# A written order of every stage in a slot of the attention heads, the rotated key's halves among the value projections, and a finer order in the odd mixer

## What is computed

```python
def mla_attend(qn, qr, kn, kr, v):            # kind A, 8 heads; kr is one rotated key for all heads
    s = einsum('bqhd,bkhd->bhqk', qn, kn) + einsum('bqhr,bkr->bhqk', qr, kr)
    p = softmax(s * scale)
    return einsum('bhqk,bkhe->bqhe', p, v)
def diff_attend(q1, q2, k1, k2, v, lam):      # kind B, 4 heads
    p = softmax(s1) - lam * softmax(s2)
    return einsum('bhqk,bkhe->bqhe', p, v)    # then rms_norm per head
for l in range(2):                            # first block
    o_a = mla_attend(lat, keys of ctx and lat); o_b = diff_attend(...)
    # in layer 0 the context's queries attend to the context too
    merged = sigmoid(ga) * (o_a @ w_br_a) + sigmoid(gb) * (rms_norm(o_b) @ w_br_b)
    x = x + gate * (merged @ w_out); x = x + gate * conv_ffn(x)
# second block: layer 0 an even mixer, layer 1 the odd mixer:
#   z = h @ w_in; compressed attention + causal attention in two branches, gated; retention; @ w_out
```

## Time and profile before

| | us |
|---|---|
| median of 3 runs | 3557.78 |
| lowest, highest | 3555.96, 3561.11 |
| profiled execution | 3556.24 |
| its span in the trace | 3554.5 |
| PE busy in it | 3348.7 |
| DVE, ACT, POOL busy | 1958.8, 1402.4, 324.9 |
| mean granted TensorE clock | 0.977 of full |

### The profile page before, as it was taken

The page is one execution under the profiler, slowest core; times in us unless marked ns, Lnnn a source line. Parts: engine busy times, 40 slices in busy tenths (PEclk is TensorE's granted clock), DMA queues, the critical chain, the costliest instruction groups (busy, mean ns, idle before and its releaser), DMA issues.

```text
span 3554.5 us, 42096 instructions
## 1 busy us (share of the span) xinstructions
PE 3348.7 (94%) x17348; PEld 2799.1 (79%) x17348; DVE 1958.8 (55%) x2880; ACT 1402.4 (39%) x2281; POOL 324.9 (9%) x269
## 2 busy tenths in 40 slices
PE   8889998999999998899899999899999989989998
PEld 5778777888888886787777888787888767768886
DVE  5675655677736635757645635555444466344343
ACT  4563443234313324544534423444222356243222
POOL 0010000221101110000011101221000210210000
PEclk9999999999999998999999999999999999999999
DMA  5001114443323322011143322222222311112222
GB/s 222 30 23 63 42 50 163 138 144 120 113 88 125 131 77 83 19 52 59 62 143 119 130 100 94 97 95 86 91 105 85 112 38 36 60 59 99 97 98 74
DMA packets 74608, 321.94 MB, mean 91 GB/s; under 512 B 9008, under 2 KB 17968, under 8 KB 52400
## 3 DMA queue, kind: packets, MB, share of 16 engines
q1 hardware_dynamic: 74416, 319.25, 25.9%
HBM read 303.49 MB, written 15.73 MB: 90 GB/s over the span
## 4 chain that ended last, share of the span: by engine, by line
PE 50%; DVE 5%; ACT 3%; issue 1%; POOL 0%; DMA 0%; DVEq 0%; ACTq 0%; POOLq 0%; SPq 0%
PE psum L688 14%; PE psum L689 14%; PE psum L690 14%; PE psum L1291 1%; DVE split_weights L658 1%; PE psum L1323 1%; ACT split_weights L640 1%; DVE arena L2158 0%; ACT arena L1437 0%; PE psum L703 0%; PE psum L3005 0%; PE psum L704 0%; PE psum L705 0%; PE psum L2590 0%; PE psum L3029 0%
## 5 line engine op out<-in xcount | busy, mean ns | idle before, releaser
L688 PE MATMUL psum<-split_inputs,split_weights 128*128 128x512 f32 (+1 forms) x2864 | 1053.8, 368 | 20.4 <-DVE split_weights L658 17.3
L689 PE MATMUL psum<-split_inputs,split_weights 128*128 128x512 f32 (+1 forms) x2864 | 1045.6, 365 | 0.0
L690 PE MATMUL psum<-split_inputs,split_weights 128*128 128x512 f32 (+1 forms) x2864 | 1044.8, 365 | 0.0
L658 DVE TENSOR_TENSOR split_weights<-arena,split_weights 128x2048 fp32r<-128x2048 f32 (+6 forms) x324 | 513.2, 1599 | 423.2 <-ACT split_weights L640 422.0
L688 PEld LDWEIGHTS psum<-split_inputs,split_weights 128*128 128x128 f32 x2864 | 543.3, 190 | 114.8 <-DVE split_weights L658 21.9
L689 PEld LDWEIGHTS psum<-split_inputs,split_weights 128*128 128x128 f32 x2864 | 543.1, 190 | 87.3 <-issue 2.8
L690 PEld LDWEIGHTS psum<-split_inputs,split_weights 128*128 128x128 f32 x2864 | 542.3, 189 | 87.0
L640 ACT ACTIVATE split_weights<-arena 128x2048 fp32r<-128x2048 f32 (+6 forms) x327 | 423.9, 1314 | 163.7 <-PE psum L690 163.6
L688 PE MATMUL psum<-split_hidden,split_weights 128*128 128x512 f32 (+1 forms) x880 | 324.3, 368 | 2.4 <-DVE split_weights L658 2.4
L689 PE MATMUL psum<-split_hidden,split_weights 128*128 128x512 f32 (+1 forms) x880 | 324.0, 368 | 0.0
L690 PE MATMUL psum<-split_hidden,split_weights 128*128 128x512 f32 (+1 forms) x880 | 323.8, 368 | 0.0
(11 more groups left out here) (354 smaller groups left out, 4773.1 us busy)
## 6 DMA issues: line engine op xcount, KB each, us to landing
arena<-w_up_dram SPq DMA_DIRECT2D x44, 1024.0 KB, 5.5
arena<-ffn_up_dram SPq DMA_DIRECT2D x44, 1024.0 KB, 4.8
arena<-w_ada_dram SPq DMA_DIRECT2D x80, 512.0 KB, 3.8
arena<-w_in_dram SPq DMA_DIRECT2D x32, 1024.0 KB, 4.8
arena<-w_down_dram SPq DMA_DIRECT2D x32, 704.0 KB, 4.1
arena<-ffn_down_dram SPq DMA_DIRECT2D x32, 704.0 KB, 4.1
arena<-od_w_in_dram SPq DMA_DIRECT2D x13, 1024.0 KB, 4.8
arena<-w_ada_dram SPq DMA_DIRECT2D x8, 1024.0 KB, 12.3
```

The lines of the kernel that those rows point to most:

```text
L658: ins = dve.e.tensor_tensor(ws[:, i, 1, cols], raw_view(key)[:, cols], ws[:, i, 0, cols].bitcast(F32), ALU.subtract)
L688: pe.e.matmul(dst, a[0], b[0], start=i == 0, stop=False)
L689: pe.e.matmul(dst, a[0], b[1], start=False, stop=False)
L690: ins = pe.e.matmul(dst, a[1], b[0], start=False, stop=i == n - 1)
```

## The change

1. `SLOT_ORDER` gives, for each layer, kind and engine, the order of twelve stages in a slot, and the loop in `head_items` follows it. Against the order before: in layer 0, kind A, PE does `values` before `turn`, ACT does `values` before `turn` and the first scores' exponential after the pieces, DVE does the pieces last. In layer 0, kind B, PE does `turn` before the first scores, DVE weighs before the first maximum and splits weights before the pieces. In layer 1, kind A, ACT does `values` before `turn`, DVE weighs first. In layer 1, kind B, PE does `ob_sum` after values, gates and pieces.
2. `PIECE_SHIFT` moves single pieces by one slot: in layer 0 both key projections of kind A one later, the latent key projection of the last three heads of kind B one earlier; in layer 1 the latent key projection of kind A one later and the context's one earlier. `GATE_AT` moves some gates by one or two slots.
3. `KRF` moves into a row of `PR`. The halves of the rotated key become four items `kr`, one behind each of the first four `v_a`, on ACT and DVE; the two waits for them ahead of L1544 go, and ACT waits for the taken latent before it writes `KRF`.
4. Odd mixer: DVE's split of the second query block moves ahead of `dve_blocks`; in `nsa_order` the weight blocks are split in quarters, one a slot, and the first of them no longer stands before the first scores; PE does `fill` ahead of `values`.

The diff. Of the loop over the slots only the first of the removed lines stand here; the rest of them are in the kernel before, printed above. Of `PIECE_SHIFT` the further entries are left out: they repeat the named ones for the other heads.

```diff
--- before.py
+++ after.py
@@ -250,8 +250,25 @@
-GATE_AT = {2: ((3, 4, 6, 7), (10, 11, 13, 14), (17, 18, 19, 20), (21, 23, 24, 26)),
-           1: ((3, 5), (7, 9), (11, 13), (15, 17))}
+GATE_AT = {2: ((3, 4, 7, 7), (10, 11, 14, 14), (17, 18, 19, 20), (22, 24, 25, 27)),
+           1: ((1, 3), (6, 9), (12, 14), (15, 17))}
+SLOT_ORDER = {
+    (0, "A", "act"): ("late", "ob_sum", "values", "turn", "ob_root", "gates", "pieces", "s0", "preps", "s1", "ob_norm", "ob_square"),
+    (0, "A", "dve"): ("s0", "late", "weigh", "turn", "ob_sum", "values", "ob_root", "gates", "preps", "s1", "pieces", "ob_norm", "ob_square"),
+    (0, "A", "pe"): ("s0", "values", "turn", "late", "ob_sum", "ob_root", "gates", "pieces", "preps", "s1", "ob_norm", "ob_square"),
+    (0, "B", "act"): ("turn", "late", "ob_sum", "values", "s0", "ob_root", "gates", "pieces", "preps", "s1", "ob_norm", "ob_square"),
+    (0, "B", "dve"): ("weigh", "s0", "late", "turn", "ob_sum", "values", "preps", "ob_root", "gates", "pieces", "s1", "ob_norm", "ob_square"),
+    (0, "B", "pe"): ("turn", "s0", "late", "ob_sum", "values", "ob_root", "gates", "preps", "s1", "pieces", "ob_norm", "ob_square"),
+    (1, "A", "act"): ("late", "ob_sum", "values", "turn", "s0", "ob_root", "gates", "pieces", "preps", "s1", "ob_norm", "ob_square"),
+    (1, "A", "dve"): ("weigh", "s0", "late", "turn", "ob_sum", "values", "ob_root", "gates", "pieces", "preps", "s1", "ob_norm", "ob_square"),
+    (1, "A", "pe"): ("s0", "turn", "late", "ob_sum", "values", "ob_root", "gates", "pieces", "preps", "s1", "ob_norm", "ob_square"),
+    (1, "B", "act"): ("turn", "late", "ob_sum", "values", "s0", "ob_root", "gates", "pieces", "preps", "s1", "ob_norm", "ob_square"),
+    (1, "B", "dve"): ("s0", "late", "weigh", "turn", "ob_sum", "values", "ob_root", "gates", "pieces", "preps", "s1", "ob_norm", "ob_square"),
+    (1, "B", "pe"): ("s0", "turn", "late", "values", "ob_root", "gates", "pieces", "ob_sum", "preps", "s1", "ob_norm", "ob_square"),
+}
+PIECE_SHIFT = {(0, 1, 2): 1, (0, 1, 3): 1, (0, 10, 3): -1,
...
@@ -358,7 +375,8 @@
         for i, step in enumerate(steps):
-            plan[lo + i * (hi - lo) // len(steps)]["pieces"].append(step)
+            x = lo + i * (hi - lo) // len(steps) + PIECE_SHIFT.get((layer, n, i), 0)
+            plan[x]["pieces"].append(step)
@@ -370,7 +388,10 @@
         if i == len(streams):
-            out += [("v_a", t) for t in range(N_TOK // P)]
+            for t in range(N_TOK // P):
+                out.append(("v_a", t))
+                if engine != "pe" and t < 4:
+                    out.append(("kr", t // 2, t % 2))
         out += step
@@ -390,42 +411,47 @@
+    def part_preps(n):
+        out.extend(preps[0:n])
+        del preps[0:n]
     for x, (i, c) in enumerate(slots):
         scores = plan[x]["scores"]
-        if engine != "act":
-            out += scores[0:1]
...
+        for stage in SLOT_ORDER[layer, pairs[i]["kind"], engine]:
+            if stage == "s0":
+                out += scores[0:1]
+            elif stage == "s1":
+                out += scores[1:]
+            elif stage == "late":
+                out += late
+                late = []
+            elif stage == "weigh":
+                out += [("weigh", t) for t in weigh]
+                weigh = []
+            elif stage == "turn":
+                out.append(("turn", i, c))
+            elif stage == "values":
+                if len(values) > 2:
+                    of_values(x, *values.pop(0))
+            elif stage == "gates":
+                if gates[x] and gates[x][0][2:] == (LAT, 0):
+                    part_preps(len(preps))
+                out += [y for y in gates[x] if y[0] != "prepare"]
+                preps += [("prepare", part, PARTS) for y in gates[x] if y[0] == "prepare" for part in range(PARTS)]
+                late += [("gate_out",) + y[1:] for y in gates[x] if y[0] == "gate"]
+            elif stage == "pieces":
+                for step in plan[x]["pieces"]:
+                    if step[0][0] == "v_b" or step[0][0] == "b_qk" and step[0][3:] == (0, LAT):
+                        part_preps(len(preps))
+                    out += [y for y in step if y[0] != "prepare"]
+                    late += [("late",) + y for y in step if y[0] in ("a_q", "a_k")]
+                    preps += [("prepare", part, PARTS) for y in step if y[0] == "prepare" for part in range(PARTS)]
+            elif stage == "preps":
+                part_preps(2)
+            else:
+                of_norm(x, stage)
+        weigh += [t for _, t in scores]
     out += late + preps
@@ -1033,7 +1059,7 @@
         OS_HI = spare(2 * P)
-        KRF = arena[:, region:region + N_TOK]
+        KRF = PR[:, 2, :]
         VB = Layout(arena, half_n0, arena_n)(6, H_B, 2 * P, words=split_words)
@@ -1105,14 +1131,9 @@
             act.wait_ge(product, "kr", l, CTX)
+            act.wait_ge(taken, "cq", l, 2, mine(l)[-1])
             act.e.activation(KRF[kr, CTX[0]:CTX[1]], banks.at("kr", l, CTX)[kr, 0:N_CTX], ACT.Copy,
                              scale=kc("scale_a")[kr, :]).then_inc(*banks.back(("kr", l, CTX), copied, "kr", l, CTX))
-            act.wait_ge(roped, l, "kr")
-            act.wait_ge(copied, "kr", l, CTX)
-            for b in range(2):
-                for at in (kr, kr2):
-                    act.e.activation(KH[at, b, 0, :], KRF[kr, :], ACT.Copy, scale=1.0 / a_scale).then_inc(
-                        *w_half("kr", l, b, at.start))
             act.wait_ge(const_in)
@@ -1145,12 +1166,6 @@
             dve.e.tensor_tensor(KRF[kr, lat], KRF[kr, lat], KT[kr, :], ALU.add).then_inc(*roped(l, "kr"))
-            for b in range(2):
-                for at in (kr, kr2):
-                    dve.wait_ge(w_half, "kr", l, b, kr.start)
-                    dve.e.scalar_tensor_tensor(out=KH[at, b, 1, :], in0=KRF[kr, :], scalar=1.0 / a_scale,
-                                               in1=KH[kr, b, 0, :].bitcast(F32), op0=ALU.mult, op1=ALU.subtract).then_inc(
-                        *taken("kr", l, b, at.start))
@@ -1396,6 +1411,12 @@
                                      ACT.Copy).then_inc(*w_half("k", l, n, s))
+                elif what == "kr":
+                    b, rows = at[0], (kr, kr2)[at[1]]
+                    act.wait_ge(roped, l, "kr")
+                    act.wait_ge(copied, "kr", l, CTX)
+                    act.e.activation(KH[rows, b, 0, :], KRF[kr, :], ACT.Copy, scale=1.0 / a_scale).then_inc(
+                        *w_half("kr", l, b, rows.start))
                 elif what == "v_a":
@@ -1538,8 +1559,6 @@
                         qt_free()
-                        dve.wait_ge(taken, "kr", l, 1, kr2.start)
-                        dve.wait_ge(w_half, "kr", l, 1, kr2.start)
                         dve.wait_ge(product, "q", l, n, s)
@@ -1560,6 +1579,12 @@
                                         ).then_inc(*banks.back(("k", l, n, s), taken, "k", l, n, s))
+                elif what == "kr":
+                    b, rows = at[0], (kr, kr2)[at[1]]
+                    dve.wait_ge(w_half, "kr", l, b, kr.start)
+                    dve.e.scalar_tensor_tensor(out=KH[rows, b, 1, :], in0=KRF[kr, :], scalar=1.0 / a_scale,
+                                               in1=KH[kr, b, 0, :].bitcast(F32), op0=ALU.mult, op1=ALU.subtract).then_inc(
+                        *taken("kr", l, b, rows.start))
                 elif what == "v_a":
@@ -2738,11 +2763,14 @@
-        def dve_odd_in(chunks):
+        def dve_odd_in(chunks, ready=0):
             block, waiting = None, []
                 if b != block:
-                    dve_prepare()
+                    if ready == 0:
+                        dve_prepare()
+                    ready = max(ready - 1, 0)
                     block = b
@@ -2958,7 +2986,8 @@
             pieces = [("fill", c, j) for c in range(len(RET_IN)) for j in range(4)]
-            out, late, evict = [("cmp_scores",), ("prepare",)], [], []
+            out, late, evict = [("cmp_scores",)], [], []
+            preps = [("prepare", part, PARTS) for part in range(PARTS)]
             for x in range(min(at.values()), len(chunk_list) + 2):
@@ -2968,17 +2997,18 @@
                     slot["fill"].append(pieces.pop(0))
-                late, evict = [], []
+                late, evict = preps[0:1] if x > -3 else [], []
+                preps = preps[len(late):]
                 for _, c, j in slot["fill"]:
                         evict += [("fill_out", c)]
-                        late += [("prepare",)] * (c % 2)
-                order = dict(pe="scores turn cmp values fill", dve="scores weigh turn cmp values late",
+                        preps += [("prepare", part, PARTS) for part in range(PARTS * (c % 2))]
+                order = dict(pe="scores turn cmp fill values", dve="scores weigh turn cmp values late",
                              act="evict turn values scores weigh cmp late")[engine]
             assert not pieces
-            return out + evict + late
```

(8 more changed lines are left out.)

32 lines of the change are left out of this document (1 added, 31 removed).

## The result

The changed kernel took 3501.9 us (median of 4 runs, 3493.8 to 3504.3) beside 3558.7 of the kernel before: ratio 0.984, 95% interval [0.982, 0.985], 56.8 us less. Run once more beside later experiments, it took 3498.0 (3491.5 to 3504.5), ratio 0.983 [0.981, 0.985], 60.8 us less. The forecast was 3507.5, in a range of 3486 to 3537.

A forecast was written before the change was run, and what follows sets the result against it. PE, busy 94% of the span, bounds the kernel, so only its waits and clock count. Terms summed to 57 us, 50 after counting the heads' 20.5 at two thirds: 3557.8 to 3507.5 us, range 3486 to 3537.

The forecast's parts named there:

- Key halves, -11.5: Starts of both layers' heads: moving KRF frees DVE's queue, so scores start 6.0 and 5.5 us sooner, -11.5 us.
- A of layer 0, -6: Layer 0's heads of kind A: the turn's wait for its weighing mostly goes in seven heads, -6 us.
- B of layer 0, -7: Layer 0's heads of kind B: shorter waits of scores (2.4), norm sums (3.9) and gates (0.7), -7 us.
- Layer 1, -4.5 and -3: Layer 1's heads: in kind A the turn's wait goes, -4.5 us; in kind B the norm sum's is covered, -3.
- Rival B: Re-ordered heads lose over half of their 73 us of idle time, 38.5, at full clock: 3483 us; chance 0.12.
- (a): Odd mixer's queries: the weight split moved ahead of the copies removes PE's wait of 4.63 us for L658, -4.6 us.
- (b): Odd mixer's first scores: without the whole block ahead of the first maximum, the 5.24 us wait shrinks to 0.8, -4.4 us.
- (c): Odd mixer's attention: fill ahead of values and quartered blocks cut PE's waits for the output bank, -8.1 us.
- The clock, -8: PE's granted clock recovers where long waits go: 5 us in the odd mixer, 3 in the heads, -8 us.
- A of the rivals: Only the starts, the odd mixer and 5 us of clock gain; the heads' re-orderings give nothing: 3524 us; chance 0.25.
- C: Heads: ACT blocks on evictions and scores wait for their bank, 2.8 us a head in 24 heads: 3591 us; chance 0.05.
- D: Moved split and fill meet the next wait at once; starts and odd mixer give half, the rest nothing: 3541; chance 0.09.

The follow-up runs named there:

- gates_back: The changed kernel with the gates back in their old slots in both layers, orders and moved pieces kept: 3510.2 us, ratio 0.9870.
- fillback: The changed kernel with the odd mixer's fill back behind the values, quarters and early block kept: 3497.7 us, ratio 0.9838.
- slots: The kernel before with only the new order of the slots, moved pieces and gates: 3520.8 us, ratio 0.9899.

## Why the prediction came out right, and where it was wrong

**Key halves, -11.5: right.** Measured -5.8 and -5.6 in the two starts, -12.0 alone. The sum by DVE's queue, from where it comes free to the last low half, gave the start of the scores at 123.3; it is 122.5, with 1.0 gained ahead. The sum didn't say that part of it would show as a higher clock rather than less idle time: 2.9 of the 6.8 in layer 0, 2.3 of the 5.6 in layer 1.

**A of layer 0, -6: too small.** Idle time fell by 7.8 and the term "0.3 of that is left a head" failed: of the 1.16 before a turn, the later exponential left nothing, except 1.3 us in two places. The caution came from one exponential that would come 3.4 us later; that its weighing would then be late for the turn was an argument, and there was room. The 0.49 before scores, which "stays", is 0.36 to 0.38 in five heads.

**B of layer 0, -7: near in sum, wrong in parts.** Norm sums: 3.5 us less, forecast 3.9. Scores: forecast 2.4 less, measured nothing. The turn between two full tiles took its 0.6 from a wait of 2.03, but in three heads and not four, and two new waits of 1.32 and 0.92 took it back; in sum 11.8 before and after. Rotations: forecast unchanged, went from 3.6 to 0.2. Gates: forecast 0.7; with the old slots of the gates the idle time is 28.4 instead of 27.9, no more than between other kernels with this order. The stretch gave 9.4 in all, near the 7 by errors that met.

**Layer 1, -4.5 and -3: A close, B at less than half.** A gave 5.3: the turn's waits for the weighing fell from 5.3 to 0.7 and a 2.5 for weights went, but the output bank's wait, which "stays", grew from 5.0 to 7.3. In B the norm sums gave 3.5, forecast 3; 1.0 of it comes back with the gates' old slots, so that the moved `ob_sum` is left with 2.5. The term that is missing is the gates': 6.1 to 6.7 us by "gates_back". I read where a gate's matmuls would fall and not where its block's quarters fall on DVE; that is the largest single miss in the heads.

**The discount.** I counted these 20.5 at two thirds, since queues feed each other. They measured 29.0 in idle time. They may feed each other, but then the follow-ups were gains as well: the stretches had waits of 94 us in sum, and a general discount had no row behind it. Rival B, which gave the heads 38.5, was nearer for them than my sum.

**The odd mixer, -17: (a) and (b) right to 0.2, (c) wrong.** The wait of 4.63 is gone, the one of 5.24 is 0.64 (forecasts -4.6 and -4.4). (c), -8.1, gave 0.4 the other way: 11.2 us of waits for the output bank became 1.0, and 10.6 of others took their place. Of these 2.1 are in the compression (L2910 for L2947, new, and L3059 for L2965, 1.4 for 0.5), to which I gave no cost; they stand in every kernel with this part, and what brings them was not tried. The step that failed is "the fill is six matmuls, 1.4 us: -5.1". It covers the bank's wait, but then it wants its own bank from ACT a turn earlier, which I didn't look up; "fillback" puts its worth at nothing, or about 1 us of loss. The quarters, for which I counted 2.6 + 2, are worth 3.8 to 4.4 of idle time beside the moved fill, and with clock 11 in the profile and 9 to 13 in the medians. But that worth isn't in the output bank's wait, where I had put it, and it makes up for what the moved fill lost.

**The clock, -8 beyond the starts: too small in this profile, right in the next.** PE's busy time fell by 8.6 us in the four stretches of heads and 5.9 in the mixer; in the second profile by 0.1 and 7.1. Five was the forecast for the mixer, three for the heads.

**So the total** came out 5.6 us from the forecast by luck, because errors met. Profile against profile the heads gave 15 us more idle time than counted and the clock 6.5 more, the starts 1 more, (c) gave 8.5 less, and the stretches outside the change 2 back. That makes 12 us more than the forecast's 50; the median has 6 of them, as the profiled execution was the fastest. The forecast's own arithmetic is off by a few tenths: 57 less a third of 20.5 is 50.2. A of the rivals fell with "slots", which alone passes it. C, by which ACT would block scores in A, would have shown in L1458: 4.3 us against 3.9. (Its price took a cost seen in kind A of layer 0 for all 24 heads; there are 8 of those.) D fell with every part.

**Its own signs.** PE's wait ahead of the value projections is 1.22 in layer 0 and none in layer 1. There is none for L658 (now L684) amid the queries, none of 5 us at the first scores and no 1.47 before norm sums. The clock at the start is 1.00 over 108 to 123 us, for 0.84. At the odd mixer's start it is 0.88 over 2829.7 to 2849.7, for 0.76, short of the 0.9 that was asked. The bank's wait is never over 0.6. PE's idle sum fell by 44, the mark was 25.

## What to carry to other kernels

Before counting a moved piece of PE work as cover for one wait, look up which bank it needs itself and who gives that back: the moved fill took away 5.8 us of one wait and made 7.8 of others. When a prefetch's due slot moves, follow the prefetch's own pieces on the vector engines, not only the matmuls. And judge such edits by idle time, which repeated within 0.8 us a stretch in two profiles of one kernel, before the median, which moved by 4 us between two groups of runs of one kernel.

## What the hardware showed that was not expected

The same order of instructions with the same waits took 451.6, 454.1 and 459.6 us in one stretch, at clocks of 0.98, 0.97 and 0.96, with idle times within 0.1 us. These executions were in three groups of runs, so whether the chip or the execution makes the difference isn't separated. Within one group, on one chip, four kernels with this order took 459.3, 459.6, 459.7 and 462.3, with 27.9 to 28.3 idle.

Where a wait went, the clock in places gave nearly as much again as the wait, or more: at the start of layer 0 4.0 us of idle time and 2.9 of busy time, in the mixer's attention, quarters against whole blocks, 3.8 and 7.7. Elsewhere it gave little or nothing: 7.8 and 1.9 in A of layer 0, 5.3 and 0.0 in A of layer 1, where the clock was 0.99 already.
The Trainium skill, "TensorE: Matmul & The Clock Gate", Part 1, has activity as what releases the throttled clock; the direction agrees with the start of layer 0, 0.84 before and 1.00 after.
